# Ranks of a token router from bf16 views, experts' places by a matrix product, an earlier half of a gather, and idle products, in a two-layer mixture-of-experts backbone

## What is computed

```python
p_coarse = softmax(x @ w_coarse); p_g, g_sel = top_k(p_coarse, 1)
fine_g = (x @ w_fine).reshape(-1, 4, 8)[token, g_sel]
top_v, top_i = top_k(fine_g, 2)
w_top = softmax(top_v) * p_g
expert = g_sel * 8 + top_i
gates = sum over the two: w_top * one_hot(expert)      # (tokens, 32)
hid = silu(x @ w1[e]) * (x @ w3[e])                    # every expert e
y = sum over e: (hid * gates[:, e]) @ w2[e]
```

## Time and profile before

| | |
|---|---|
| three runs, median | 1211.0 us (1209.51 to 1213.44) |
| the profiled execution, its own time | 1205.39 us |
| its span in the trace | 1203.6 us |
| PE, DVE, ACT busy | 91%, 52%, 38% of the span |
| mean granted clock of PE | 0.97 of full speed |

### The profile page before, as it was taken

The page is one execution under the profiler, slowest core; times in us unless marked ns, Lnnn a source line. Parts: engine busy times, 40 slices in busy tenths (PEclk is TensorE's granted clock), DMA queues, the critical chain, the costliest instruction groups (busy, mean ns, idle before and its releaser), DMA issues.

```text
span 1203.6 us, 18067 instructions
## 1 busy us (share of the span) xinstructions
PE 1093.1 (91%) x6840; PEld 769.3 (64%) x6840; DVE 620.0 (52%) x1230; ACT 456.0 (38%) x818; POOL 66.9 (6%) x113
## 2 busy tenths in 40 slices
PE   4999999999979799998969999999997988999983
PEld 0767777887766455564548777778775655555552
DVE  0644767788554522222267575678866254222224
ACT  0634554454242223332344344636523322333322
POOL 0401000201000000000020000010000000000000
PEclk8899999999989999999989999999997999999997
DMA  9997865545999999999766887546376799999990
GB/s 352 303 334 258 302 252 174 169 158 193 374 396 394 410 409 409 409 409 407 282 179 213 305 289 271 175 150 210 126 280 263 261 409 409 409 409 408 409 364 35
DMA packets 107982, 360.11 MB, mean 299 GB/s; under 512 B 9220, under 2 KB 12768, under 8 KB 99696
## 3 DMA queue, kind: packets, MB, share of 16 engines
q1 hardware_dynamic: 97392, 301.48, 65.9%
q0 software_dynamic: 10496, 57.39, 13.8%
HBM read 356.13 MB, written 3.74 MB: 299 GB/s over the span
## 4 chain that ended last, share of the span: by engine, by line
PE 62%; DVE 15%; ACT 7%; issue 6%; DMA 4%; DVEq 3%; ACTq 1%; SPq 0%
PE bank L920 59%; PE bank L923 3%; DVE wl L1865 3%; ACT wh L1540 3%; DMA first<-in_w_ada 2%; ACT hidT L1812 2%; DMA raw<-in_w_in 1%; DMA adaw<-in_w_ada 1%; DVE merged L1865 1%; DVEq L2214 1%; DVE tmp L1865 1%; DVE tmp L2198 1%; DVE seg L2338 1%; DVE xbc L2133 0%; DVE xbc L2130 0%
## 5 line engine op out<-in xcount | busy, mean ns | idle before, releaser
L1865 DVE TENSOR_TENSOR wl<-raw,wh 128x2048 fp32r<-128x2048 f32 (+1 forms) x76 | 169.2, 2236 | 63.0 <-ACT wh L1540 61.6
L1540 ACT ACTIVATE wh<-raw 128x2048 fp32r<-128x2048 f32 (+1 forms) x76 | 142.4, 1876 | 70.0 <-PE bank L920 48.6
L920 PE MATMUL bank<-raw,xg 128*64 128x256 f32 x1088 | 125.9, 382 | 7.5 <-issue 7.5
L920 PE MATMUL bank<-wh,hTh 128*128 128x512 f32 x448 | 126.2, 404 | 0.5 <-ACT merged L1562 0.5
L920 PEld LDWEIGHTS bank<-raw,xg 128*64 128x64 f32 x1088 | 92.9, 138 | 47.1 <-issue 25.6
L920 PE MATMUL bank<-wh,hTl 128*128 128x512 f32 x448 | 121.0, 392 | 0.0
L920 PE MATMUL bank<-wl,hTh 128*128 128x512 f32 x448 | 120.0, 390 | 0.0
L920 PE MATMUL bank<-wide,xg 128*64 128x256 f32 x1024 | 117.6, 381 | 0.0
L2507 DVE TENSOR_SCALAR selT<-bank 128x256 fp32r<-128x256 f32 x66 | 28.0, 425 | 168.7 <-ACTq L1787 168.7
L920 PEld LDWEIGHTS bank<-wide,xg 128*64 128x64 f32 x1024 | 89.0, 138 | 36.7 <-issue 16.3
L2597 DVE SCALAR_TENSOR_TENSOR hid<-bank,gg,sil 128x128 f32<-128x128 f32 x66 | 23.1, 350 | 148.6 <-ACT sil L1810 147.6
(11 more groups left out here) (326 smaller groups left out, 1480.9 us busy)
## 6 DMA issues: line engine op xcount, KB each, us to landing
raw<-in_moe_w SPq DMA_DIRECT2D x136, 512.0 KB, 10.8
wide<-in_moe_w SPq DMA_DIRECT2D x128, 512.0 KB, 11.2
raw<-in_w_in SPq DMA_DIRECT2D x52, 1024.0 KB, 6.6
wide<-in_moe_w SPq DMA_DIRECT2D x34, 1024.0 KB, 11.7
adaw<-in_w_ada POOLq DMA_DIRECT2D x32, 1024.0 KB, 6.6
raw<-in_moe_w SPq DMA_DIRECT2D x32, 1024.0 KB, 11.9
raw<-in_w_branch SPq DMA_DIRECT2D x12, 1024.0 KB, 5.4
raw<-in_w_ada SPq DMA_DIRECT2D x8, 1024.0 KB, 9.8
```

The lines of the kernel that those rows point to most:

```text
L920: return behind(nc.tensor.matmul(*args, **kw))
L1540: A_(wh[c][:, 0:n], raw[:, r, 0:n], ACT.Copy).then_inc(part_high[c], 1)
L1865: return V.tensor_tensor(o, a, b, op)
```

## The change

- **Ranks and counts.** The masks are read as bf16: the upper half of each f32 word, which is exact for 0 and 1. Two products first give `count`, the tokens of each expert, as a 32 x 128 block in bank 0. DVE copies it to `tmp` and signals (so `experts_chosen` counts twice a layer). Three bf16 products give each token's rank among its expert's tokens, itself counted, and two f32 products of `tmp` with a 32 x 32 mask add the experts' opening places in the same bank. The five doublings are gone.
- **Offsets for later use.** Three more products put the opening places and totals in bank 1 (`offset`). DVE fetches them in `places`, behind `build(0)` and three `low_rows`.
- **Selection.** A token's two places count from 1, so `build` compares with the numbers 1 to 256, and `iota` is one column longer. One step makes the second place from the first. `sel_built` is signalled after each stream.
- **Gather.** The first half goes through the high parts of stream 0, then of stream 1, each after its own signal. The banks waited for ahead of it are those of `count`, `offset`, `x200` and `rank`.
- **DVE's order.** `low_rows(1, 0)` moves from ahead of the ranks to behind `build(0)`.
- **Idle products.** Eight (`busy5`) in both layers instead of five in the last, and in the last layer twelve more (`busy_chosen`) ahead of the wait for the mask.

```diff
         plan.append(("busy3", 4))
         plan.append(("busy4", 4))
-        plan.append(("busy5", 4))
+        plan.append(("busy_chosen", 4))
+    plan.append(("busy5", 4))
...
+    plan.append(("count", 0))
     plan.append(("rank", 5))
+    plan.append(("offset", 1))
...
-    out["iota"] = np.tile(np.arange(float(HALF_ROOM)), (P, 1))
+    out["iota"] = np.tile(np.arange(HALF_ROOM + 1.0), (P, 1))
...
-                pe.wait_ge(experts_chosen, l + 1)
+                if l == L - 1:
+                    keep_busy(l, "busy_chosen", 12)
+                pe.wait_ge(experts_chosen, 2 * l + 1)
+                def ones_high(ap):
+
+                    return ap.bitcast(BF16).rearrange("p (n h) -> p n h", h=2)[:, :, 1]
+
+                picked = [ones_high(chosen[:, s, 0:NE]) for s in range(2)]
+                ones = ones_high(C["rev4"][:, 3:4]).to_broadcast([P, P])
+                upto = ones_high(C["upto"])
+                t = bank_free(pe, l, "count")
+                mm(t[0:NE, 0:P], picked[0], ones, start=True, stop=False)
+                fills(mm(t[0:NE, 0:P], picked[1], ones, start=False, stop=True), "count")
                 t = bank_free(pe, l, "rank")
-                picked = [chosen[:, s, 0:NE] for s in range(2)]
-                ones = C["rev4"][:, 3:4].to_broadcast([P, P])
-                mm(t[:, 0:32], C["before"], picked[0], start=True, stop=True)
-                mm(t[:, 32:64], ones, picked[0], start=True, stop=False)
-                mm(t[:, 32:64], C["before"], picked[1], start=False, stop=True)
-                mm(t[:, 64:96], ones, picked[0], start=True, stop=False)
-                ins = mm(t[:, 64:96], ones, picked[1], start=False, stop=True)
+                add(t[:, 0:NE], upto, picked[0], start=True)
+                add(t[:, NE:2 * NE], ones, picked[0])
+                add(t[:, NE:2 * NE], upto, picked[1])
+                counts = tmp[0:NE, 0:P]
+                before = C["before"][0:NE, 0:NE]
+                pe.wait_ge(experts_chosen, 2 * l + 2)
+                for s in range(2):
+                    ins = add(t[:, s * NE:(s + 1) * NE], counts, before, stop=s == 1)
                 fills(ins, "rank")
-                if l == L - 1:
-                    keep_busy(l, "busy5", 5)
+                t = bank_free(pe, l, "offset")
+                mm(t[:, 0:NE], counts, before, start=True, stop=True)
+                mm(t[:, NE:2 * NE], ones, picked[0], start=True, stop=False)
+                fills(mm(t[:, NE:2 * NE], ones, picked[1], start=False, stop=True), "offset")
+                keep_busy(l, "busy5", 8)
...
-                def pick(h, c, part, opens, last):
+                def pick(h, s, c, part, opens, last):
                     out = bank[GATHER_BANKS[c // 2]][:, (c % 2) * HALF_ROOM:(c % 2 + 1) * HALF_ROOM]
+                    return add(out, part[:, s, c * P:(c + 1) * P], sel[:, s, h * HALF_ROOM:(h + 1) * HALF_ROOM], start=opens, stop=last)
+
+                def gather():
+
+                    pe.wait_ge(x2_high, 4 * (l + 1))
+                    for name in ("count", "offset", "x200", "rank"):
+                        bank_emptied(pe, l, name)
                     for s in range(2):
-                        ins = add(out, part[:, s, c * P:(c + 1) * P], sel[:, s, h * HALF_ROOM:(h + 1) * HALF_ROOM],
-                                  start=opens and s == 0, stop=last and s == 1)
-                    return ins
-
-                def gather():
-
-                    pe.wait_ge(x2_high, 4 * (l + 1))
-                    for name in ("wo00", "wo01", "x200", "rank"):
-                        bank_emptied(pe, l, name)
-                    pe.wait_ge(sel_built, 2 * l + 1)
-                    for c in range(DC):
-                        pick(0, c, x2h, c % 2 == 0, False)
+                        pe.wait_ge(sel_built, 4 * l + s + 1)
+                        for c in range(DC):
+                            pick(0, s, c, x2h, s == 0 and c % 2 == 0, False)
                     for c in range(DC):
                         if c % 4 == 0:
                             for s in range(2):
                                 bank_emptied(pe, l, f"x2{s}{c // 4}")
-                        ins = pick(0, c, x2l, False, c % 2 == 1)
+                        for s in range(2):
+                            ins = pick(0, s, c, x2l, False, s == 1)
                         if c % 2:
                             ins.then_inc(gathered_, 1)
-                    pe.wait_ge(sel_built, 2 * l + 2)
+                    pe.wait_ge(sel_built, 4 * l + 4)
                     for c in range(DC):
                         if c % 2 == 0:
                             pe.wait_ge(room_filled, 2 * QUARTERS * l + c // 2 + 1)
-                        pick(1, c, x2h, c % 2 == 0, False)
-                        ins = pick(1, c, x2l, False, c % 2 == 1)
+                        for s in range(2):
+                            pick(1, s, c, x2h, s == 0 and c % 2 == 0, False)
+                        for s in range(2):
+                            ins = pick(1, s, c, x2l, False, s == 1)
...
+                t = bank_full(dve, l, "count")
+                frees(V.tensor_copy(tmp[0:NE, 0:P], t[0:NE, 0:P]), "count")
+                drain().then_inc(experts_chosen, 1)
                 low_rows(0, 0)
-                low_rows(1, 0)
-                t = bank_full(dve, l, "rank")
-                V.tensor_copy(total[0][:, NE // 2:], t[:, 64:96])
-                drain()
-                for n in range(5):
-                    a, b = total[n % 2], total[1 - n % 2]
-                    tt(b[:, NE // 2:], a[:, NE // 2:], a[:, NE // 2 - (1 << n):NE // 2 + NE - (1 << n)], ALU.add)
-                    drain()
-                frees(tt(offset[:, :], total[1][:, NE // 2:], t[:, 64:96], ALU.subtract), "rank")
-                drain()
                 def of_streams(n):
                     return pair[:, :, n:n + 1]
-                V.scalar_tensor_tensor(out=posx[:, :, :], in0=t[:, 0:64].rearrange("p (s e) -> p s e", s=2), scalar=1.0,
-                                       in1=bc(offset[:, :], 1, 2), op0=ALU.add, op1=ALU.add)
-                V.tensor_copy(place[:, :, 0:NE], t[:, 0:64].rearrange("p (s e) -> p s e", s=2))
+                t = bank_full(dve, l, "rank")
+                ranks = t[:, 0:2 * NE].rearrange("p (s e) -> p s e", s=2)
+                tt(posx[:, :, :], ranks, chosen[:, :, 0:NE], ALU.mult)
+                frees(V.tensor_copy(place[:, :, 0:NE], ranks), "rank")
                 drain()
-                tt(posx[:, :, :], posx[:, :, :], chosen[:, :, 0:NE], ALU.mult)
+                V.tensor_reduce(of_streams(2), posx[:, :, :], X, ALU.max)
+                V.tensor_reduce(of_streams(0), posx[:, :, :], X, ALU.add)
                 drain()
-                V.tensor_reduce(of_streams(0), posx[:, :, :], X, ALU.max)
-                V.tensor_reduce(of_streams(1), posx[:, :, :], X, ALU.add)
-                drain()
-                V.tensor_scalar(of_streams(2), of_streams(0), -1.0, None, ALU.add)
-                V.scalar_tensor_tensor(out=of_streams(3), in0=of_streams(1), scalar=-1.0, in1=of_streams(0), op0=ALU.add, op1=ALU.subtract)
-                drain()
-                for n in (2, 3):
-                    V.tensor_scalar(of_streams(n + 2), of_streams(n), -float(HALF_ROOM), None, ALU.add)
+                tt(of_streams(3), of_streams(0), of_streams(2), ALU.subtract)
                 def build(h):
                     hs = slice(h * HALF_ROOM, (h + 1) * HALF_ROOM)
+                    seats = C["iota"][:, 1:1 + HALF_ROOM]
                     for s in range(2):
-                        V.tensor_scalar(sel[:, s, hs], C["iota"], pair[:, s, 2 + 2 * h:3 + 2 * h], None, ALU.is_equal)
+                        V.tensor_scalar(sel[:, s, hs], seats, pair[:, s, 2 + 2 * h:3 + 2 * h], None, ALU.is_equal)
                     drain()
                     for s in range(2):
-                        ins = V.scalar_tensor_tensor(out=sel[:, s, hs], in0=C["iota"], scalar=pair[:, s, 3 + 2 * h:4 + 2 * h],
-                                                     in1=sel[:, s, hs].bitcast(F32), op0=ALU.is_equal, op1=ALU.add)
-                    ins.then_inc(sel_built, 1)
+                        V.scalar_tensor_tensor(out=sel[:, s, hs], in0=seats, scalar=pair[:, s, 3 + 2 * h:4 + 2 * h],
+                                               in1=sel[:, s, hs].bitcast(F32), op0=ALU.is_equal, op1=ALU.add).then_inc(sel_built, 1)
+
+                def places():
+
+                    t = bank_full(dve, l, "offset")
+                    V.tensor_copy(offset[:, :], t[:, 0:NE])
+                    frees(V.tensor_copy(total[:, :], t[:, NE:2 * NE]), "offset")
+                    drain()
+                    V.scalar_tensor_tensor(out=place[:, :, 0:NE], in0=place[:, :, 0:NE], scalar=-1.0, in1=bc(offset[:, :], 1, 2),
+                                           op0=ALU.add, op1=ALU.subtract)
...
                 run = mains[l]
                 build(0)
```

(9 more changed lines are left out.)

4 lines of the change are left out of this document (2 added, 2 removed).

## The result

The changed kernel takes **1191.1 us** (median of five runs, 1184.9 to 1192.7) against 1209.5 for the kernel before on the same chips (five runs, 1208.2 to 1213.4). The ratio is 0.983, 95% interval 0.981 to 0.986.

A forecast was written before the change was run, and what follows sets the result against it. It took PE as the bound in the items and DVE's chain between mask and gather. Earlier starts of 1.8 us plus clock gains of 2.4 and 0.7 made 4.9: 1211.0 to 1206.1 us, range 1202.5 to 1210.0.

The forecast's parts named there:

- the early signal of stream 0: Before the gather: stream 0's selection signalled at 339.1, but the gather waits for bank 1 until 341.88, so no gain.
- Rival 4: The gather does start on stream 0's signal, 2.7 us earlier in each layer: 1200.7 us; chance 0.02.
- Layer 0's start: The gather's start from the shorter path: 0.3 us sooner in layer 0, 1.5 in layer 1.
- rival 3: Idle products hold up real work: layer 1's twelve end 2.67 us behind the mask; 1211.9 us, chance 0.07.
- a draw: After 2.8 us of PE idle before the gather, keeping the full clock is somewhat better than even.
- kept in both: Full clock at the gather in both layers: 1.8 + 4.76 = 6.6 us gained.
- The middle that I forecast: Clock kept at the gather in one layer, lost in the other: 1.8 + 2.4 + 0.7 = 4.9 us gained.
- A lost clock: At the gather, a layer keeping the clock gains 2.33 or 2.43 us; one losing it 0 to 1.4, taken as 0.7.
- doubt about the comparison's start: In the selection, reading from `iota`'s second column might slow the comparison, 0.54 us in all; taken as nothing.
- the sum itself: Whole kernel: start 1.8 us plus the clock's gain, likeliest 4.9 us, with items still 7.23 us apart.
- No cost: Weight loads in the items: an earlier start of 1 to 3 us eats into 13 us of room, costing nothing.

The follow-up runs named there:

- e5: The changed kernel with the openings in bank 4 and the eight idle products in bank 1, swapped; ratio to the kernel before 0.980.
- e6: The changed kernel with 28 semaphore increments on DVE between items 8 and 27 of layer 1; ratio to the kernel before 0.980.
- e3: The changed kernel with 15 and 13 semaphore increments on DVE, putting its later code where the kernel before has it; ratio to before 0.986.
- e10: The changed kernel run again, nothing altered; 1189.1 us, ratio to the kernel before 0.982.
- e7: The kernel before with harmless increments on PE and DVE, giving it the changed kernel's code positions; ratio to before 0.9872.
- e11: e7 once more, beside the changed kernel on the same chip; 1196.6 us against 1210.7 before, ratio 0.9869.
- e1: The kernel before with 23 and 37 semaphore increments on PE ahead of its wait for the mask; ratio to before 0.987.
- e4: The kernel before with 12 semaphore increments at the start of PE's program; 1200.6 us in one run.
- e8: The kernel before with 128 semaphore increments at the start of PE's program; 1198.5 us in one run.
- e9: The changed kernel with the changes of e5 and e6, and on DVE `build(1)` ahead of the places; 1183.3 us, ratio to before 0.977.

## Why the prediction was wrong

**The mechanisms that it named for its stretch were right.** The bound between mask and gather was DVE's chain; the early signal of stream 0 bought nothing as written, because bank 1 came back last (e5 shows it: give that bank to the idle products, and the gather starts 2.4 us sooner). Rival 4 is out. Layer 0's start gained 0.4 us (6.55 to 6.14; I had 0.3), layer 1's 1.8 (7.94 to 6.14; 1.5). In the profile after, the twelve idle products ended before the mask, 1.48 us ahead of the first count (I had 1.5), and turning back in layer 1 ran at full speed, 1.94 us. So rival 3 didn't happen there; e6 shows that it can, at 0.6 us.

**The clock.** I called 2.8 us of idle a draw, and it is one. In the first profile it was 2.70 in layer 0, and the full clock held; in layer 1 the clock fell behind the openings and was back before the gather. So the case "kept in both", 6.6 us, came true there (6.4 in the sections). But of the eight gathers in the profiles of the change with this PE code (the first, e3, e6, e10), four begin at full clock, with item 0 after 19.4 to 19.7 us, and four at the low one, after 20.9 to 21.0. The middle that I forecast was fair, and the first profile was lucky. A lost clock costs 1.2 to 1.6 us there, near the difference of 1.6 and 1.7 that I had between 2.33 or 2.43 and 0.7. The 0.54 us of doubt about the comparison's start came to nothing: two still take 0.61 us. The sentence of the Trainium skill on alignment (Vector Engine (DVE) Microarchitecture Reference, section 5.1) is no more than not contradicted, since both starts lie on 4-byte boundaries.

**The step that failed is the sum itself: it took everything outside the stretch as unchanged.** I said that the items are 7.23 us apart and that PE has no room in them. This holds for the two that I looked at the earlier trace rows, not for item 28 in either layer. The missing terms are -6.1 and -5.0 us (item 28), about -5 us (DVE ahead of layer 1: 323.0 against 317.8 in e7) and +2.8 us (the end): -13.5 us together, and e11 measured 14.1. They depend on how many instructions the change adds and where, which the order of instructions would have let me count, though not which of the stops would go and which would come. And there was a sign: the chain gave 6% of the span to "issue", 72 us for which no engine is to blame. The four gaps of before shown above are 14.4 us of these. I read over that share.

**Weights.** No cost was right for item 28 and after. A few items around the sixth to ninth take 8.5 to 10.9 us in every kernel here, so "PE has no room" did not hold there even before the change: the earlier trace rows has PE waiting 1.92 us for DVE's `hid` in one of them. The stretch that holds them changed by up to 1.5 us either way (-1.16 and +1.54 in the table), which I had not priced.

## What to carry to other kernels

When a change gains or loses more than its own stretch explains, split both traces at the same instructions, and look for idle time with "issue" as its end just behind branches and at far-off places. Then test it by moving code with harmless instructions in a place where the engine waits anyway: it costs one run and tells what the change itself is worth. Take what the clock is worth at a place from several profiles, not from one. Before forecasting a change to a kernel with branches, count the instructions that it adds on each engine ahead of them, and take every such gap of the trace before as a term that may go, or come.

## What the runs showed of the hardware

- An engine can stand still for its own instructions: PE 1.0 to 4.1 us at or behind a taken branch; DVE 5.3 to 6.0 us early in layer 1 (before, e1, e3, e4, e8) or 2.6 to 2.8 near the end (all others but e6 and e9). The Trainium skill (Runtime: NRT & Kernel Launch, Instruction fetch mechanics) says that a taken branch whose target is not in the window already fetched makes the engine wait for the load of that page, and that code comes in blocks of 16 KiB, 256 instructions. The first agrees with before's layer 1, where the branch took 4.31 us. It does not fit the other nine branches of PE in before, the changed kernel, e1, e4 and e8, which took 0.4 to 0.5 us, though their targets too lie 1179 instructions on; the program announces each of them ahead by `branch_hint`. The second agrees for PE (58 loads, 0.95 MB), not for the other engines, whose loads are 8 KB (36 of them, 0.29 MB). The block behind the target should, by the same section of the Trainium skill, be fetched while the current one runs; in layer 0 of before it was asked for only after PE had stopped.

  Page before, the same two lines:

```profile
q8 instruction: 58, 0.95, 0.3%
q14 instruction: 36, 0.29, 0.1%
```

- The stall moves with the code as a step, not a slope: 23 instructions more, and 6 us were gone.
- Both gaps on DVE move with the number of its instructions (e3, e6, e7), and one lies well into the next layer. Counted in DVE's program from 0, the instruction that comes late is number 961 in before and e3, 1857 in the changed kernel (the wait just ahead of `root`) and 2113 in e7: 7 and 9 times 128 further on. Why DVE stops at these places and not at every 128th instruction is open. Why one cost 5.9 us and the other 2.7 is open; other transfers filled the queues in the first and none ran in the second, a possible reason that was not tried.
- The time to the first count of layer 0 went from 335.2 to 342.3 us between executions of kernels that have the same code up to there. One profile against one other is worth no more than that; the stretch from item 28 to the last repeats to 0.02 us in all of them but e4's layer 1.
